# Hybrid attention and mixture-of-experts layer: the stretch from the first norm to the first expert's gate-up, rearranged

## Chip, core and metric

The kernel runs on one core of one Trainium2 chip. The metric is the device time of one execution in microseconds: 1241.69 is the median of three runs of the kernel before (1239.27 to 1242.06).

## The reference

One decoder layer over 256 tokens of width 1024, all in float32: a mixer of three attention kinds, a LayerNorm, 32 experts of which each token uses 4, and a LayerNorm. What matters here, cut down:

```python
mix = hybrid_mixer(x, ...)
x = layer_norm(DEEPNORM_ALPHA * x + mix, ln1_g, ln1_b)
logits = x @ router_w + router_b                     # 256 x 32
top_logit, top_e = lax.top_k(logits, 4)
top_w = softmax(top_logit)
for e in range(32):                                  # tokens routed to e
    gu = xb @ w_gu[e] + b_gu[e]                      # 1024 x 2048 weights, 8 MB
    gate, up = minimum(gu[:, :1024], 7), clip(gu[:, 1024:], -7, 7)
    y = (gate * sigmoid(1.702 * gate) * (up + 1)) @ w_dn[e] + b_dn[e]    # 4 MB
    out[tokens] += y * w[:, None]
x = layer_norm(DEEPNORM_ALPHA * x + out, ln2_g, ln2_b)
```

## The kernel before

The program is written by hand, one stream of instructions per engine with explicit semaphores; there is no scheduler. The tokens are two blocks b of 128. The five streams are SP (weight loads, from line 290), POOL (403), ACT (487), TensorE (712) and VectorE (1171). All of TensorE's products but a few pass through the helper at line 716 and its transposes through lines 723, 947, 964, 1048 and 1053, so that rows must be told apart by shape. A float32 product appears as two matmul instructions, a float32 transpose as one.

**Weights.** Two buffers hold gate-up weights (8 MB each, in four chunks of 2 MB, for even and odd experts), one holds down weights (4 MB, in four chunks). SP loads those of experts 0 and 1 ahead (line 326), as far as the buffers are free, the down weights of expert 0 after the last output projection (line 331), and then loops over pairs of experts: each chunk is loaded again when TensorE has used it (`guc`, `dn_used`), extra blocks included (`xguc`, `xdnc`, with an offset of four). Before the loop SP waits for the semaphore `routed`.

**Experts.** An expert takes up to 64 tokens in its slots. The products run over 64 stationary columns in two column groups. An expert with more tokens gets extra blocks of 32 slots, with 32 stationary columns in four column groups; the number per expert, `nx`, is computed on the chip. Expert 1 has one such block in this data.

**From the norm to the first gate-up** (the stretch of the change):

- The output projections give 12 pieces; VectorE adds each to `y` (`add_mixed`, line 1395), for block 0 up to piece 7, for block 1 up to piece 11. Pieces 8 and 10 belong to block 1's first half.
- `norm` (1411) takes statistics of both halves (1413, 1414), aggregates (1416), adds epsilon (1417), multiplies by the gain (1419) while POOL computes the power -1/2 (478, or 482 in the final norm), and applies deviation and bias (1421), which signals `x1ok`.
- TensorE transposes x block by block (947, eight each), ACT copies to `x1T` (609, two halves of a block). Then the router: eight products per block with x1T as the stationary operand (128 columns) and 32 moving columns, both blocks behind both blocks' transposes.
- VectorE clears `CTx` and `ysb` (1429, 1430) behind the norm. Per block it adds the bias (1436), finds the top 8 and their indices (1437, 1438), subtracts the maximum (1439; ACT then takes the exponential, 615), and makes a 0/1 mask (1440 to 1443).
- TensorE counts tokens per expert with five products of `before` and the mask (written to PB2).
- VectorE normalises the routing weights (1448 to 1452), computes `nx` in six operations from the counts (1457, 1460), then the slot number of each token (1463, 1464; `routed`), and the one-hots of experts 0 and 1: `oh`, and `ohw` with the routing weight (1473, 1474), eight operations, signalled by `ohs`.
- TensorE transposes the routing weights (964), gathers the tokens of experts 0 and 1 with 16 products (32 instructions) in two halves, clears the output accumulators with eight bf16 products of zeros, and starts the gate-up. ACT copies both halves of the gather (625); the gate-up waits for the second.
- After the first gate-up: activation on VectorE (1498 to 1504) and ACT (659), four transposes (1048), two of `ohw` (1053), and `combine`, the first product into the accumulators: bias of the down projection by routing weight.

## Time and profile before

| | |
|---|---|
| median of three runs | 1241.69 us |
| the profiled execution | 1241.96 us, of which span 1240.2 us |
| TensorE busy | 1101.1 us (89%) |
| VectorE busy | 266.9 us (22%) |
| ACT, POOL busy | 146.2 and 30.1 us |
| HBM read | 424.91 MB, 343 GB/s over the span |
| chain that ended last | TensorE 50%, transfers 29%, SP's queue 14%, VectorE 3%, issue 2% |

The page cuts the span into 40 slices of 31 us. A slice in which transfers move some 418 GB/s is one in which they are busy all the time; TensorE's 89% doesn't make it the bound there, since its matmuls wait within such a slice too. TensorE's granted clock has two levels here, 1.00 (2.4 GHz) and 0.50 (1.2 GHz); a stretch with a value between them has some of both. Ends of matmuls are modelled, so starts are read rather than ends where a row allows it.

### The profile page before, as it was taken

To read this page: it belongs to the slowest core of one execution; us is meant where nothing else is said; L and a number is where in the kernel's file an instruction comes from. 1 tells how busy PE (TensorE), PEld (TensorE's weight loads), DVE (VectorE), ACT (ScalarE), POOL (GpSimd) and SP (SyncE) were. 2 spreads that over 40 slices of the span, in tenths; PEclk is the share of its full clock that TensorE was granted. 3 is DMA by queue.
4 is the path that set the end of the run, shared out by engine and by line. 5 is a ranking of instruction groups with operands and counts; after the bars stand their busy time and mean duration, and the time that the engine had idled before them with its cause. 6 is when DMAs were issued, how large, how long until landed. Compare 5 with 4: busy or idle time off the path is not lost.

```text
span 1240.2 us, 14598 instructions
## 1 busy us (share of the span) xinstructions
PE 1101.1 (89%) x5388; PEld 474.5 (38%) x5389; DVE 266.9 (22%) x767; ACT 146.2 (12%) x309; POOL 30.1 (2%) x53
## 2 busy tenths in 40 slices
PE   7999796998899998989898878999989898989883
PEld 6677445333234332323232332433333232323221
DVE  2354535111112111121111111111211111111113
ACT  2144311100001000001000001001000010100000
POOL 3000410000000000000000000000000000000000
PEclk9999896998899999999999998999999999999997
DMA  9400849730999999999999958999999999999993
GB/s 314 181 1 1 262 191 393 294 137 17 419 419 418 419 418 418 418 417 417 418 419 418 418 232 326 418 417 418 417 418 418 418 418 418 419 418 418 417 414 120
DMA packets 80435, 426.32 MB, mean 344 GB/s; under 512 B 6025, under 2 KB 7610, under 8 KB 47610
## 3 DMA queue, kind: packets, MB, share of 16 engines
q1 hardware_dynamic: 79834, 425.37, 84.8%
q10 hardware_dynamic: 576, 0.61, 0.2%
q8 instruction: 16, 0.26, 0.1%
q14 instruction: 9, 0.07, 0.0%
HBM read 424.91 MB, written 1.05 MB: 343 GB/s over the span
## 4 chain that ended last, share of the span: by engine, by line
PE 50%; DMA 29%; SPq 14%; DVE 3%; issue 2%; ACT 1%; POOL 0%; DVEq 0%; POOLq 0%; ACTq 0%
PE PB L716 48%; DMA WB<-in_w_gate_up_dram 22%; SPq L331 6%; DMA WB<-in_w_down_dram 6%; SPq L326 6%; PE PB L1048 0%; DMA X<-in_x_dram 0%; SPq L335 0%; DVE S L1395 0%; PE PB L723 0%; DVE S L1524 0%; POOL K L478 0%; DVE WB L1289 0%; PE PB L806 0%; DVE S L1504 0%
## 5 line engine op out<-in xcount | busy, mean ns | idle before, releaser
L716 PE MATMUL PB<-WB,S 128*64 128x512 f32 (+5 forms) x3472 | 775.0, 596 | 72.3 <-DMA WB<-in_w_gate_up_dram 62.6
L716 PEld LDWEIGHTS PB<-WB,S 128*64 128x64 f32 (+2 forms) x3472 | 250.0, 140 | 562.8 <-issue 410.5
L1498 DVE TENSOR_SCALAR S<-PB 128x512 f32<-128x512 f32 (+1 forms) x34 | 23.5, 692 | 604.8 <-PE PB L716 604.8
L716 PE MATMUL PB<-S 32*64 32x512 f32 (+5 forms) x464 | 113.7, 594 | 4.9 <-issue 2.5
L659 ACT ACTIVATE S<-S 128x512 f32<-128x512 f32 x32 | 20.2, 630 | 556.4 <-DVE S L1498 556.4
L716 PE MATMUL PB<-S,X 128*128 128x128 f32 (+1 forms) x576 | 75.7, 293 | 9.3 <-DVE S L1524 8.0
L716 PEld LDWEIGHTS PB<-S,X 128*128 128x128 f32 x576 | 72.4, 208 | 23.7 <-issue 21.9
L716 PEld LDWEIGHTS PB<-S 32*64 32x64 f32 (+4 forms) x464 | 41.6, 164 | 65.0 <-issue 58.0
L1542 DVE COPY S<-PB 64x512 f32<-64x512 f32 x32 | 21.9, 683 | 205.4 <-PE PB L716 205.4
L716 PE MATMUL PB<-S,WB 128*128 128x256 f32 (+2 forms) x336 | 63.7, 391 | 0.4 <-ACT S L498 0.4
L716 PEld LDWEIGHTS PB<-S,WB 128*128 128x128 f32 (+1 forms) x336 | 49.5, 178 | 12.5 <-issue 2.1
L716 PE MATMUL PB<-WB 128*32 128x128 f32 (+7 forms) x260 | 44.7, 362 | 5.2 <-DVE WB L1362 3.3
L675 ACT ACTIVATE S<-PB 64x512 f32<-64x512 f32 x32 | 19.0, 593 | 203.0 <-PE PB L716 203.0
L716 PEld LDWEIGHTS PB<-WB 128*64 128x64 f32 (+2 forms) x260 | 27.5, 152 | 18.7 <-issue 13.7
L482 POOL TENSOR_TENSOR K<-K 128x1 f32<-128x1 f32 x2 | 3.0, 1511 | 1038.4 <-DVE K L1417 1038.4
L1048 PE MATMUL PB<-K,S 128*128 128x128 f32 x128 | 21.5, 292 | 4.7 <-DVE S L1504 2.9
L1048 PEld LDWEIGHTS PB<-K,S 128*128 128x128 f32 x128 | 13.7, 143 | 30.7 <-issue 26.9
L1501 DVE SCALAR_TENSOR_TENSOR S<-S 128x512 f32<-128x512 f32 (+1 forms) x34 | 23.5, 691 | 1.2
L1504 DVE TENSOR_TENSOR S<-S 128x512 f32<-128x512 f32 (+1 forms) x34 | 23.5, 691 | 1.2
L1499 DVE TENSOR_SCALAR S<-PB 128x512 f32<-128x512 f32 (+1 forms) x34 | 23.2, 682 | 0.1
L625 ACT ACTIVATE S<-PB 128x512 f32<-128x512 f32 x32 | 19.1, 597 | 32.7 <-PE PB L716 32.7
L1473 DVE TENSOR_SCALAR S<-K 128x64 f32<-128x64 f32 x68 | 17.1, 251 | 21.6 <-PE PB L1053 19.5
(199 smaller groups left out, 339.4 us busy)
## 6 DMA issues: line engine op xcount, KB each, us to landing
WB<-in_w_gate_up_dram SPq DMA_DIRECT2D x128, 2048.0 KB, 22.8
WB<-in_w_down_dram SPq DMA_DIRECT2D x128, 1024.0 KB, 23.0
WB<-in_w_in_dram SPq DMA_DIRECT2D x1, 3088.0 KB, 15.2
WB<-in_w_in_dram SPq DMA_DIRECT2D x1, 3072.0 KB, 20.3
WB<-in_w_in_dram SPq DMA_DIRECT2D x1, 2144.0 KB, 11.1
WB<-in_w_in_dram SPq DMA_DIRECT2D x1, 2048.0 KB, 16.1
WB<-in_w_out_dram SPq DMA_DIRECT2D x2, 1024.0 KB, 10.2
WB<-in_w_out_dram SPq DMA_DIRECT2D x1, 2048.0 KB, 16.7
```

The lines of the kernel that those rows point to most:

```text
L326: sp.dma_start(gu_slot[par][:, kk * c:kk * c + kk, :], src[:, kk * c:kk * c + kk, :]).then_inc(s_gul[par][c], 16)
L331: sp.dma_start(dn_slot[:, kk * c:kk * c + kk, :], src[:, kk * c:kk * c + kk, :]).then_inc(s_dnl[par][c], 16)
L625: act.activation(xg[:, 4 * h:4 * h + 4, :].rearrange("p k s -> p (k s)"), PB[bank][:, :], ACT.Copy)\
L659: act.activation(act_sb, gt, ACT.Sigmoid, scale=SWIGLU_ALPHA).then_inc(s["sig"], 1)
L675: act.activation(ysb[64 * e:64 * e + 64, 1, :], PB[7][64:128, :], ACT.Copy).then_inc(s["ysb_ok"], 1)
L716: return mm_(o, l, r, start=start, stop=stop, skip_group_check=True)
L1048: ins = tr(PB[bank][:, P * c:P * c + P], act_sb[:, P * c:P * c + P], ident)
L1498: ts(g, gate, LIMIT, None, ALU.min).then_inc(s[g_ok], 1)
L1499: ts(u, up, LIMIT, -LIMIT, ALU.min, ALU.max).then_inc(s[clip], 1)
L1501: stt(u, u, 1.0, g, ALU.add, ALU.mult).then_inc(s[upg], 1)
L1504: tt(a, u, a, ALU.mult).then_inc(s[done], 1)
L1542: cp(ysb[64 * e:64 * e + 64, 0, :], PB[7][0:64, :]).then_inc(s["ysb_dv"], 1)
```

## The change

**Norm.** The first half's statistics are taken before the last addition of a block (which only touches the second half), and the two wide operations are split into halves; `x1ok` is signalled per half, and TensorE transposes a half as soon as it is signalled. POOL's code serves both norms with one semaphore.

**Router.** Block 0's router stands before block 1's transposes. Weights are now the stationary operand (32 columns) and x1T moves (128 columns); k and k+4 accumulate in column group k, so that four partial sums of the transposed logits stand in four partition groups. ACT copies them (`lgT`), and one product with `fold`, four identities of 32 stacked, adds and transposes them back. VectorE builds `fold` at the start of the program with three additions.

**Routing.** VectorE signals the mask before it subtracts the maximum. It clears buffers between the two blocks. Three of the five count products are issued after block 0's mask. From the counts come first the slot numbers, for both blocks in two operations; then `oh` for both experts in one comparison, `ohs`; then `nx` (`nx_ok`), the routing weights (`wts_ok`), and `ohw` straight from `posm` and `wts`.

**Moved.** `ysb` is cleared by POOL. The transposes of the routing weights and the clearing of the accumulators stand behind the first gate-up, and ACT's copy of those weights behind its first sigmoid. The initial counts of `xguc` and `xdnc` come from the transposes. SP waits for `nx_ok` in place of `routed`.

```diff
@@ SP
-            sp.wait_ge(s["routed"], 1)
+            sp.wait_ge(s["nx_ok"], 1)
@@ POOL
...
+            for b in range(TB):
+                reciprocal_deviation(b)
+            pool.wait_ge(s["x1ok"], 2 * TB)
+            pool.memset(ysb, 0.0).then_inc(s["ysbz"], 1)
@@ ACT
+                act.wait_ge(s["lgp"], b + 1)
+                act.activation(lgT[:, b, :], PB[b][:, 0:P], ACT.Copy).then_inc(s["lgc"], 1)
+
+            act.wait_ge(s["ysbz"], 1)
+            act.dma_start(ysb[0:N_EXPERTS, :, :], b_dn[0].rearrange("e (h d) -> e h d", h=2)).then_inc(s["bdn_ld"], 16)
             for b in range(TB):
                 act.wait_ge(s["ract"], b + 1)
                 act.activation(lg[:, b, :], lg[:, b, :], ACT.Exp).then_inc(s["rsum"], 1)
...
             sigmoid(1)
+            act.wait_ge(s["wt_ps"], 1)
+            act.wait_ge(s["ctz"], 1)
+            act.activation(CT[0:N_EXPERTS, :, :].rearrange("p b t -> p (b t)"), PB[7][0:N_EXPERTS, 0:256],
+                           ACT.Copy).then_inc(s["ysb_ok"], 1)
             act_columns(5, 1)
             combine_weights(1)
+            act.wait_ge(s["nx_ok"], 1)
@@ TensorE
             for b in range(TB):
-                pe.wait_ge(s["x1ok"], b + 1)
-                if b == 1:
-                    pe.wait_ge(s["ymix"], 12)
                 for h in range(2):
+                    pe.wait_ge(s["x1ok"], 2 * b + h + 1)
+                    if b == 1 and h == 0:
+                        pe.wait_ge(s["ymix"], 12)
...
                     ins.then_inc(s["x1t"], 1)
-            for b in range(TB):
-                pe.wait_ge(s["x1tsb"], 2 * b + 2)
+                if b == 0:
+                    pe.wait_ge(s["ymix"], 11)
+
                 for k in range(KT):
-                    ins = mm(PB[b][:, 0:N_EXPERTS], x1T[:, k, P * b:P * b + P], rw[:, k, :], k == 0, k == KT - 1)
-                ins.then_inc(s["lgt"], 1)
-
-            pe.wait_ge(s["route"], 2)
+                    if k % 4 == 0:
+                        pe.wait_ge(s["x1tsb"], 2 * b + k // 4 + 1)
+                    q = 32 * (k % 4)
+                    ins = mm(PB[b][q:q + 32, 0:P], rw[:, k, :], x1T[:, k, P * b:P * b + P], k < 4, k >= 4)
+                ins.then_inc(s["lgp"], 1)
+                pe.wait_ge(s["lgc"], b + 1)
+                mm(PB[b][:, 256:256 + N_EXPERTS], lgT[:, b, :], fold, True, True).then_inc(s["lgt"], 1)
+
+            pe.wait_ge(s["route"], 1)
             mm(PB[2][:, 0:32], before[:, 0:P], msk[:, 0, :], True, False)
             mm(PB[2][:, 32:64], before[:, P:256], msk[:, 0, :], False, False)
+            mm(PB[2][:, 64:96], before[:, P:256], msk[:, 0, :], False, False)
+            pe.wait_ge(s["route"], 2)
             mm(PB[2][:, 32:64], before[:, 0:P], msk[:, 1, :], False, False)
-            mm(PB[2][:, 64:96], before[:, P:256], msk[:, 0, :], False, False)
             mm(PB[2][:, 64:96], before[:, P:256], msk[:, 1, :], False, True).then_inc(s["cntp"], 1)
...
             gate_up(0, 1, 1)
+            expert_weight_transposes()
+            clear_outputs()
             act_transposes(5, 1)
@@ VectorE
+            link(tt(fold, ident[:, 0:32], ident[:, 32:64], ALU.add))
+            link(tt(fold, fold, ident[:, 64:96], ALU.add))
+            tt(fold, fold, ident[:, 96:128], ALU.add).then_inc(s["foldok"], 1)
...
             for b in range(TB):
-                for n in ((6, 7), (8, 9, 10, 11))[b]:
+                for n in ((6,), (8, 9, 10))[b]:
                     add_mixed(n)
+                dve.wait_ge(s["ymix"], (7, 11)[b])
+                link(half_stats(y, b, 0))
+                add_mixed((7, 11)[b])
                 dve.wait_ge(s["ymix"], (8, 12)[b])
-                norm(y, None, b, "lnstat", "lnp", 48, lng, lnb, x_sb, "x1ok", "ln_ld")
-            dve.wait_ge(s["x1ok"], 2)
-            dve.memset(CTx, 0.0)
-            dve.memset(ysb, 0.0).then_inc(s["ysz"], 1)
+                link(half_stats(y, b, 1))
+                for ins in norm(y, b, b + 1, lng, lnb, x_sb, "ln_ld"):
+                    ins.then_inc(s["x1ok"], 1)
...
+            dve.wait_ge(s["x1ok"], 2 * TB)
+            route(0)
+            dve.memset(CTx, 0.0).then_inc(s["ctxz"], 1)
...
+            route(1)
+            dve.wait_ge(s["cntp"], 1)
             dve.wait_ge(s["route"], 2)
+            pm = posm[:, 0:N_EXPERTS, :].rearrange("p e b -> p b e")
+            link(stt(pm, PB[2][:, 0:2 * N_EXPERTS].rearrange("p (b e) -> p b e", b=TB), -NOT_ROUTED, msk, ALU.add, ALU.mult))
+            ts(pm, pm, NOT_ROUTED, None, ALU.add).then_inc(s["routed"], 1)
+            dve.wait_ge(s["routed"], 1)
+
+            tt(oh.rearrange("p b (e s) -> p b e s", e=2), iota_s.unsqueeze(1).unsqueeze(1).broadcast_to([P, TB, 2, SLOTS]),
+               posm[:, 0:2, :].rearrange("p e b -> p b e").unsqueeze(3).broadcast_to([P, TB, 2, SLOTS]), ALU.is_equal)\
+                .then_inc(s["ohs"], 1)
...
+            ins.then_inc(s["nx_ok"], 1)
```

## Rows read from the trace of the kernel before

**Rows 1.** The page's 40 slices of 31 us: transfers' busy tenths, and bytes moved.
```profile
DMA  9400849730999999999999958999999999999993
GB/s 314 181 1 1 262 191 393 294 137 17 419 419 418 419 418 418 418 417 417 418 419 418 418 232 326 418 417 418 417 418 418 418 418 418 419 418 418 417 414 120
```

**Rows 2.** Chain of waits, in order of time: start us, us, what.
```profile
423.33 27.92 DMA WB<-in_w_gate_up_dram
```

**Rows 3.** Timeline, weight loads that SP issues: start us, us issuing, queue, line.
```profile
178.77 2.63 SPq L326 DMA_DIRECT2D WB<-in_w_gate_up_dram  x5
...
307.05 6.41 SPq L326 DMA_DIRECT2D WB<-in_w_gate_up_dram  x4
```

**Rows 4.** Timeline, 182 to 220 us: start, us, engine, line, out<-in, shape, count [idle].
```profile
182.97 0.69 DVE L1413 BATCH_NORM_STATS2 K<-S 128x6 f32<-128x512 f32 x1
...
183.58 0.68 DVE L1414 BATCH_NORM_STATS2 K<-S 128x6 f32<-128x512 f32 x1
...
194.45 1.28 DVE L1421 SCALAR_TENSOR_TENSOR X<-S,K 128x1024 f32<-128x1024 f32 x1 [0.52 <-POOL K L478]
...
195.79 1.97 PE L947 MATMUL PB<-K,X 128*128 128x128 f32 x8 [5.91 <-DVE X L1421]
...
197.55 6.87 PE L716 MATMUL PB<-S 128*128 128x32 f32 x32
...
204.46 0.19 DVE L1436 TENSOR_TENSOR K<-PB,K 128x32 f32<-128x32 f32 x1 [1.70 <-PE PB L716]
...
206.23 2.34 PE L716 MATMUL PB<-K 128*128 128x32 f32 x10 [1.81 <-DVE K L1443]
...
208.68 0.19 DVE L1457 TENSOR_SCALAR K<-PB 128x32 f32<-128x32 f32 x1 [0.44 <-PE PB L716]
...
212.76 5.53 PE L716 MATMUL PB<-S,X 128*128 128x128 f32 x32 [1.35 <-DVE S L1474]
...
218.13 1.04 PE L716 MATMUL PB<-S 128*128 128x256 bf16 x8
...
218.33 0.60 ACT L625 ACTIVATE S<-PB 128x512 f32<-128x512 f32 x1 [1.19 <-PE PB L716]
...
219.10 13.95 PE L716 MATMUL PB<-WB,S 128*64 128x512 f32 x64
```

**Rows 5.** Timeline, other places: instructions of the shapes that the change adds.
```profile
37.89 3.69 PE L716 MATMUL PB<-WB 128*32 128x128 f32 x64
...
58.63 0.42 DVE L1275 TENSOR_TENSOR WB<-WB 128x256 f32<-128x256 f32 x1
...
128.79 0.74 POOL L458 MEMSET WB<- 128x768 f32 x1 [117.51 <-PE PB L716]
...
242.95 0.38 ACT L670 ACTIVATE S<-PB 128x256 f32<-128x256 f32 x1 [4.27 <-PE PB L716]
...
257.68 3.84 PE L716 MATMUL PB<-S,X 128*128 128x128 f32 x32
...
303.19 9.69 PE L716 MATMUL PB<-WB,S 128*32 128x512 f32 x64 [0.47 <-ACT S L638]
```

**Rows 6.** Timeline, end of the first gate-up, and the transposes behind it.
```profile
232.98 0.21 PEld L716 LDWEIGHTS PB<-S 32*64 32x64 f32 x8 [0.81 <-issue]
...
236.94 1.12 PE L1048 MATMUL PB<-K,S 128*128 128x128 f32 x4 [2.86 <-DVE S L1504]
```

**Rows 7.** Busy time by stretch; PEclk is the granted clock as a share.
```profile
core 0: us, PE busy (x) PEld busy (x) DVE busy (x) ACT busy (x) POOL busy (x), PEclk, DMA share, GB/s
...
191.00:193.00 2.00, 0.00 (x0) 0.00 (x0) 1.91 (x5) 0.07 (x1) 0.18 (x1) 0.86 1.05 434
...
205.00:207.00 2.00, 0.77 (x4) 0.77 (x4) 1.71 (x11) 0.23 (x1) 0.00 (x0) 0.50 1.02 426
...
215.00:217.00 2.00, 2.00 (x14) 2.00 (x13) 0.00 (x0) 0.45 (x1) 0.00 (x0) 0.66 1.02 403
...
238.00:242.00 4.00, 4.00 (x10) 2.01 (x9) 1.64 (x8) 0.60 (x1) 0.00 (x0) 0.72 1.00 418
```

**Rows 8.** Timeline, VectorE at the start of the program.
```profile
9.00 0.69 DVE L1182 COPY S<-PB 128x512 f32<-128x512 f32 x1 [1.01 <-PE PB L723]
```

More of the change, by code:

```diff
@@ L123, in hybrid_layer @@
         fg, fb = reg_a[:, 0:D], reg_a[:, D:2 * D]
-        K = sb("K", 1170)
+        K = sb("K", 1202)
         take = carver(K[:, :])
@@ L146, in hybrid_layer @@
         before = take(2 * P)
+        fold = take(N_EXPERTS)
         idx8 = sb("idx8", TB * 8, U32)
@@ L615, in _ @@
                 act.activation(lg[:, b, :], lg[:, b, :], ACT.Exp).then_inc(s["rsum"], 1)
-            act.wait_ge(s["ysz"], 1)
-            act.dma_start(ysb[0:N_EXPERTS, :, :], b_dn[0].rearrange("e (h d) -> e h d", h=2)).then_inc(s["bdn_ld"], 16)
-            act.wait_ge(s["wt_ps"], 1)
-            act.wait_ge(s["ysz"], 2)
-            act.activation(CT[0:N_EXPERTS, :, :].rearrange("p b t -> p (b t)"), PB[4][0:N_EXPERTS, 0:256],
-                           ACT.Copy).then_inc(s["ysb_ok"], 1)
             def slots_to_sbuf(h, bank, n):
@@ L1430, in _, with route @@
-            dve.memset(ysb, 0.0).then_inc(s["ysz"], 1)
-            dve.memset(posm[:, N_EXPERTS:, :], NOT_ROUTED)
-            dve.memset(wts[:, N_EXPERTS:, :], 0.0)
-            for b in range(TB):
+                link(half_stats(y, b, 1))
+                for ins in norm(y, b, b + 1, lng, lnb, x_sb, "ln_ld"):
+                    ins.then_inc(s["x1ok"], 1)
+            def route(b):
                 dve.wait_ge(s["lgt"], b + 1)
-                link(tt(lg[:, b, :], PB[b][:, 0:N_EXPERTS], rb, ALU.add))
+                link(tt(lg[:, b, :], PB[b][:, 256:256 + N_EXPERTS], rb, ALU.add))
@@ L1484, in next_expert_rows @@
                 expert_rows(e)
-            cp(curp, posm[:, 0:2, :].rearrange("p e b -> p (e b)")).then_inc(s["xact"], 1)
-            cp(curw, wts[:, 0:2, :].rearrange("p e b -> p (e b)"))
-            dve.memset(ecnt[:, 0:1], 0.0)
-            link(dve.memset(ecnt[:, 1:2], 1.0))
-            one_hots(0)
+            for e in range(2):
+                for b in range(TB):
+                    ins = ts(ohw[:, b, 64 * e:64 * e + 64], iota_s, posm[:, e, b:b + 1], wts[:, e, b:b + 1],
+                             ALU.is_equal, ALU.mult)
+            ins.then_inc(s["xact"], 1)
             expert_rows(0)
@@ L1591, in _ @@
                 link(ins)
-                norm(yf, None, b, "fin", "flnp", 32, fg, fb, yf, "fout", "ln2_ld")
+                half_stats(yf, b, 0)
+                link(half_stats(yf, b, 1))
+                for h, ins in enumerate(norm(yf, b, TB + b + 1, fg, fb, yf, "ln2_ld")):
+                    if h == 1:
+                        ins.then_inc(s["fout"], 1)
     return nc
```

111 lines of the change are left out of this document (63 added, 48 removed).

## Prediction

> **What bounds the kernel now.** I read the page's slices first. The bytes moved per slice stand at 417 to 419 GB/s from the eleventh slice (310 us) to the end, but for one dip, and at 294, 137 and 17 GB/s in slices 8 to 10 (217 to 310 us) [rows 1]. So the kernel has two regimes: a head in which the weight buffers are full and transfers wait for the engines, and a long tail in which the transfers set the pace. The chain of waits says the same: its first long piece that is a transfer of expert weights stands at 423.33, 27.92 us of gate-up weights [rows 2]; such pieces follow at every second expert, and ahead of it the long pieces are TensorE's. The question for an edit in the head is what starts the tail. SP's issues answer it: the prefetch of gate-up weights for experts 0 and 1 goes out at 178.77 (five chunks of 2 MB), and the load of expert 3, with which the unbroken stream begins, is issued at 307.05 [rows 3]. That load waits for TensorE's extra block of expert 1, whose gate-up starts at 303.19 [rows 5]. Between the first gather and that moment TensorE is in the chain throughout. Whatever brings the first gate-up forward by n us brings 307.05 forward by n, and the whole stream behind it.
>
> The stretch that the change touches runs from 182 to 219 us. In order of time: the first LayerNorm's statistics for token block 0 start at 182.97; the last operation of the norm for block 1 runs 194.45 to 195.73; eight transposes of block 1 take 195.79 to 197.76; the router's 32 matmul instructions run 1.97 to 6.87 us more (197.55 to 204.42); routing of block 1 on VectorE starts at 204.46; the count matmuls run from 206.23; VectorE then reads them at 208.68; the first gather starts at 212.76 and the first gate-up at 219.10 [rows 4]. TensorE was idle for 5.9 us, 1.8 us and 1.35 us before the transposes, the counts and the gather: this is a chain of dependences with short work on each engine, so durations on it count in full.
>
> **The norm.** Today both halves' statistics follow the last addition, 0.61 us apart (182.97 and 183.58 [rows 4]). The change takes the first half's statistics ahead of the last addition, which for block 0 waits for its output projection anyway: block 0 is done 0.6 us sooner. Block 1's additions follow on VectorE directly, so it inherits this; there a statistics operation merely swaps places with an addition and gets one wait of its own more, so I keep 0.5 us. Then the last operation is split in halves and the first half alone lets the transposes start: half of the 1.28 us [rows 4], 0.64. Start of block 1's transposes: 195.79 - 0.5 - 0.63 = 194.66. The other split operation waits for POOL's power in any case, and two halves 0.61 us apart cost what one whole does, so they are put at nothing.
>
> **The router.** Today block 0's router stands behind block 1's transposes on TensorE. The change puts it before them, in VectorE's norm of block 1, where TensorE sits idle for 5.9 us [rows 4]; it and its copy end near 193, so it leaves the path: half of 6.87 us. Block 1's router is on the path in a new form. Its 8 products become 16 instructions with 32 stationary and 128 moving columns, in four column groups. The nearest row in shape took 3.69 us for 64, 58 ns each, in two groups at the high clock [rows 5]. The granted clock here is the low level (0.50, that is 1.2 GHz, in 205 to 207 [rows 7]), so I take 115 ns each, 1.85 us. Bounds: no overlap at all, as for a 128-column transpose or today's router instruction, 0.215 us each (6.87/32), 3.4 us; from the four-group row, 9.69 us for 64 instructions of 512 columns [rows 5], a quarter of its 151 ns and doubled for the clock, 1.2 us. Changing the tile shape costs too: before the 32x64 matmuls the weight load stood for 0.81 us [rows 6], of which some 0.3 us are the pace of the stream itself, so I charge 0.5 us for the one switch between transposes and router; the switch to the fold lies under ACT's copy. Then come two steps that are new: ACT's copy of the partial sums (128x128; the 128x256 copy is 0.38 us [rows 5], I take 0.3), and the fold, one product of two instructions as today's router has them, 0.43 us. With a last instruction's 0.2 us and 0.05 us for a hand-over each: transposes to 196.63, switch to 197.15, router to 199.2 with its tail, copy to 199.55, fold to 200.25. ACT's x1T copies of 0.60 us [rows 4] run beside: the second half is there by 197.3, when TensorE is still at k 0 to 3. Today the result stands at 204.42, so 4.2 us are saved here, of which 1.13 come from the norm.
>
> The Trainium skill, page "TensorEngine Tiling (Array Packing)", section "Key Properties", says that a change of tiling mode drains TensorE, which speaks against this change with its two switches per block. The 0.81 us row agrees with it as to sign; by that rule alone both switches of block 1 would lie open, and the sum would be 0.5 us less favourable. The Trainium skill, page "TensorE: Matmul & The Clock Gate", section "Measured speedup vs the span model", has groups run side by side, with about 4 ns for each further one. The two-group row, 58 ns against the 120 ns of a full-width gather instruction of as many columns (3.84/32 [rows 5]), agrees for two; by that page four groups would need half of that again, block 1's router an estimated 0.9 us and not 1.85, and the sum would be 0.9 us better.
>
> **Routing.** VectorE takes 206.23 - 204.46 = 1.77 us from the logits to the mask today [rows 4]; the subtraction in the middle moves behind the mask, 0.15 us off: 200.3 + 1.62 gives 201.9. Of the ten count instructions, 2.45 us to VectorE's next step (208.68), six depend on block 0 alone and are issued beforehand; four remain: 2.45 - 6 x 0.215 = 1.16 us, to 203.1. Today 4.08 us follow between 208.68 and the gather: the chain of six overflow counts, positions in two pairs, two copies and eight one-hot operations. Of these the change leaves three ahead of the gather: two over 64 columns, near the 0.19 us of the 32-column row [rows 4], and one 128x256 comparison like the 0.42 us row [rows 5]; with hand-overs 0.95 us. Gather at 204.0, against 212.76: 8.8 us sooner. The memsets on VectorE between the blocks (0.5 us) lie in its wait for block 1's router, from about 197 to 200.
>
> **What is moved off.** The 4 KB-wide memset of ysb goes to POOL, idle here; 768 columns took it 0.74 us [rows 5]. ACT waits for it before it issues the b_down load and computes the exponentials. Queued behind are the gather's copies at 208, 11 us later; hidden. The routing weights (four operations per block), the overflow counts and the weighted one-hots now run under the gather and first gate-up (over 20 us). SP waits for the overflow counts rather than the positions, ready at about 205, and its next load needs the first gate-up chunk anyway. The eight clearing bf16 products (1.04 us) stood under ACT's copy of the gather's second half, so that their removal there gains nothing: the gate-up still follows that copy (218.33, 0.60 us; gate-up 219.10 [rows 4]). They and the two weight transposes now go behind the first gate-up, where TensorE waits for the activation up to 236.94 [rows 6], 2.8 us: about 1.5 us, hidden. ACT's copy of these weights falls between its sigmoid and the transposes. If that cover were gone they would cost 1.5 us once. They may also give something: in today's gap the clock falls, and 238 to 242 runs at 0.72 of the full clock [rows 7], so 2.2 us at the low level, a loss of 1.1 us; filled, the gap may keep the clock. Between 0 and 1.1 I take 0.5. The three fold additions at the start of the program shift VectorE by about 0.6 us, while its second copy waits 1.01 us for TensorE [rows 8]: nothing. The final norm is cut in halves also; nothing.
>
> **The sum.** 8.8 + 0.5 = 9.3 us. The weights don't take it back: the five chunks from 178.77 are 10 MB, some 25 us at 419 GB/s [rows 1, 3], and the first gate-up would start at 210.3, its last chunk's partner later still. The profiled execution took 1241.96 us, 1.8 us more than its span, and it gives 1232.7; it lies 0.3 us above the median of the runs, 1241.69. Predicted: 1232.5 us.
>
> **Rivals.** (a) The clock stays up. It was at 1.00 until 191 and fell after TensorE's idle time (0.86 in 191 to 193 [rows 7]); now TensorE has the router in that idle time. At the high level the transposes cost 1 us, router, fold and counts 1.7 us less, and the gather 3.84 us as the later one does [rows 5] and not 5.53: 4.3 us, so 1228.2. For it: the work moved in; against it: this work is thin, and the busy router of today, 6.87 us without a pause, didn't raise the clock. 18%. (b) The router gains little: instructions one after the other, 1.6 us more, the rise of the clock after the gather and not in it (32 x 0.215 - 5.53 = 1.35 us), and no gain in the gap, 0.5: 3.5 us, 1236.0. Today's clock rose in the gather (215 to 217 at 0.66 [rows 7]), against it. 15%. (c) The end doesn't move, since transfers set it: 1241.7. Against it stands the idle time of the transfers in slices 8 to 10. 3%. (d) Slower: the thinned stretch leaves the clock at the low level well into the expert products. Each us of gate-up at that level loses 0.5; to eat the 9.3 us it would have to last 19 us, and 24 us to be slower by the 2.5 us that can be told. With 30 us it gives 1247.5. The rise in the gather within 4 us speaks against it. 2%. That leaves 62% for the forecast.
>
> **Numbers.** (a) and (b) together give 1228.2 to 1236; the worst of the unknown costs in (b) plus the clearing products uncovered, 1.5 us, give 1237.5. The range is 1228 to 1237.5, which leaves out (c), (d) and rare sums. Under 0.2% (2.5 us, about what a measurement of this kernel tells from no change): forecast, (a) and (b) are faster, 95%; (c) 3%; (d) 2%.
>
> **What to look at.** Block 1's transposes at 194.7; 32 router instructions of 32 stationary columns, near 0.115 us; fold near 200; gather at 204.0; gate-up 0 at 210.3; expert 3's first load at 298; span 1231. Wrong if the gather comes after 206, or if it comes in time and 307.05 moves by less than it.

## The result, and the profile after

The changed kernel takes 1225.86 us (median of 4 executions, 1225.25 to 1226.71), the kernel before 1240.48 in the same series. The ratio is 0.9883, with an interval of 0.9866 to 0.99: 14.6 us less. Forecast were 9.3 us less, 1232.5, with a range down to 1228.0. The direction was right, the size was not, and the time lies below the range.

The profiled execution took 1225.68 us, its span 1223.9, against 1240.2. Its page, the slices of 30.6 us:

```profile
DMA  9400759834999999999999939999999999999993
GB/s 315 187 1 1 231 206 386 332 139 181 418 418 417 418 417 418 417 418 417 418 418 418 418 144 409 417 418 417 418 418 417 419 417 418 418 418 418 418 414 122
```

The picture is that of [rows 1]. The stream still runs unbroken at 417 to 419 GB/s from the eleventh slice, with one dip; only what lies ahead of it has become shorter. The timeline of the changed stretch, from the last addition of block 0 (start us, us, engine, line, out<-in, shape, count, idle time and its releaser):

```profile
181.26 0.75 DVE L1426 SCALAR_TENSOR_TENSOR S<-PB,K,S 128x512 f32<-128x512 f32 x1 [0.29 <-PE PB L726]
...
189.74 0.82 PE L726 MATMUL PB<-S 128*32 128x128 f32 x16 [0.84 <-ACT S L616]
...
190.96 1.41 DVE L1453 SCALAR_TENSOR_TENSOR S<-S,K 128x512 f32<-128x512 f32 x2
...
191.12 0.99 POOL L483 TENSOR_TENSOR K<-K 128x1 f32<-128x1 f32 x1 [6.89 <-DVE K L1449]
...
192.40 1.42 DVE L1458 SCALAR_TENSOR_TENSOR X<-S,K 128x512 f32<-128x512 f32 x2
...
193.21 1.88 PE L958 MATMUL PB<-K,X 128*128 128x128 f32 x8 [1.84 <-DVE X L1458]
...
195.01 0.20 PEld L726 LDWEIGHTS PB<-S 128*32 128x32 f32 x8 [0.33 <-ACT S L616]
...
195.02 1.41 PE L726 MATMUL PB<-S 128*32 128x128 f32 x16
...
196.49 0.28 ACT L620 ACTIVATE S<-PB 128x128 f32<-128x128 f32 x1 [0.77 <-PE PB L726]
...
196.82 0.41 PE L726 MATMUL PB<-K,S 128*128 128x32 f32 x2 [0.40 <-ACT S L620]
...
197.34 0.19 DVE L1473 TENSOR_TENSOR K<-PB,K 128x32 f32<-128x32 f32 x1 [1.39 <-PE PB L726]
...
198.96 0.63 PE L726 MATMUL PB<-K 128*128 128x32 f32 x4 [1.06 <-DVE K L1479]
...
200.12 0.42 DVE L1497 TENSOR_TENSOR S<-K 128x256 f32<-128x256 f32 x1
...
200.60 5.25 PE L726 MATMUL PB<-S,X 128*128 128x128 f32 x32 [1.01 <-DVE S L1497]
...
206.53 13.95 PE L726 MATMUL PB<-WB,S 128*64 128x512 f32 x64 [0.69 <-ACT S L630]
...
224.36 0.66 PE L1065 MATMUL PB<-K,S 128*128 128x128 f32 x4 [1.66 <-DVE S L1560]
...
254.29 0.66 PE L1065 MATMUL PB<-K,S 128*128 128x128 f32 x4
...
291.09 6.30 SPq L328 DMA_DIRECT2D WB<-in_w_gate_up_dram  x4
```

The row at 193.21 answers to 195.79 of [rows 4], the one at 197.34 to 204.46, the gather at 200.60 to 212.76, the gate-up at 206.53 to 219.10, the row at 224.36 to 236.94 of [rows 6], and the load of expert 3 at 291.09 to 307.05 of [rows 3]. Cut at such landmarks, the two profiled executions and a second one of each kernel (first two runs of the next section) compare as follows, in us:

| stage | forecast gain | before | before again | after | after again |
|---|---|---|---|---|---|
| start to last addition, block 0 | 0 | 182.19 | 182.07 | 181.26 | 180.77 |
| to block 1's transposes | 1.13 | 13.60 | 13.60 | 11.95 | 11.95 |
| to VectorE's reading of the logits | 3.03 | 8.67 | 8.67 | 4.13 | 4.44 |
| to the gather | 4.6 | 8.30 | 8.30 | 3.26 | 3.70 |
| to the first gate-up | 0 | 6.34 | 6.36 | 5.93 | 6.35 |
| first bias product to second gate-up | 0.5 | 9.79 | 9.81 | 8.18 | 9.88 |
| down 0 to the next gate-up | 0 | 9.49 | 9.53 | 7.60 | 7.60 |
| final norms, first to last wide operation | 0 | 11.96 | 11.96 | 11.53 | 11.53 |

Of the stages left out, the first gate-up takes 13.89 in all and the way from the second gate-up to down 0 18.67; from the gate-up behind down 0 to expert 3's load it is 36.1, 36.1, 36.2 and 37.0, and from that load to the end 933.2, 932.8, 932.8 and 930.5. The first row of the table is luck: it lies between 177.7 and 182.3 over the profiled executions of all versions. The differences that return in both pairs are 1.65 + about 4.4 + about 4.8 + 1.9 + 0.4 = 13.2 us; the gap behind the first gate-up gives 1.6 more in one pair and nothing in the other. The first gate-up also starts 0.4 us sooner after the gather in the first pair (the clock), and in the second pair the stage ahead of expert 3's load takes 0.8 more. So between the last addition of block 0 and expert 3's load the first pair gains 15.0 us and the second 11.5; of the second pair's 15.1 us in all, 3.6 lie ahead of and behind the chain that was changed. Two things stand out against the forecast: the router gives more than 3.0, and 1.9 us vanish between down 0 and the next gate-up, where the change has touched nothing.

Two stretches of the changed kernel (start and end, length, busy us and count on PE, PEld, DVE, ACT and POOL, granted clock, transfers' share, GB/s):

```profile
201.00:203.00 2.00, 2.00 (x11) 2.00 (x11) 1.73 (x12) 0.00 (x0) 0.00 (x0) 0.50 1.01 371
...
226.00:230.00 4.00, 4.00 (x15) 1.43 (x15) 0.97 (x5) 0.38 (x1) 0.00 (x0) 1.00 1.01 420
```

The gather still runs at 1.2 GHz for its first half, as before; behind the gap, where the kernel before stood at 0.72 [rows 7], it is at 2.4 GHz now.

### The profile page after: what moved, and what is told of

Same layout as the page of the kernel before. It is cut to its first block, busy times and chain, and to the rows that moved or that the text cites. A ratio compares the mean times of both kernels' runs of the same rounds, so it can differ in the third digit from the quotient of the medians.

```text
span 1223.9 us, 14619 instructions
## 1 busy us (share of the span) xinstructions
PE 1094.2 (89%) x5392; PEld 466.8 (38%) x5393; DVE 266.5 (22%) x770; ACT 146.8 (12%) x311; POOL 29.2 (2%) x54
## 4 chain that ended last, share of the span: by engine, by line
PE 48%; DMA 28%; SPq 17%; DVE 4%; issue 2%; ACT 1%; DVEq 0%; ACTq 0%
PE PB L726 47%; DMA WB<-in_w_gate_up_dram 23%; SPq L333 9%; SPq L328 6%; DMA WB<-in_w_down_dram 5%; DMA X<-in_x_dram 0%; PE PB L1065 0%; DVE S L1453 0%; DVE K L1443 0%; SPq L337 0%; DVE S L1426 0%; PE PB L733 0%; DVE S L1580 0%; DVE S L1645 0%; DVE WB L1320 0%
## 5 line engine op out<-in xcount | busy, mean ns | idle before, releaser
L726 PE MATMUL PB<-S 32*64 32x512 f32 (+5 forms) x464 | 107.7, 588 | 5.8 <-issue 2.5
L726 PEld LDWEIGHTS PB<-S 32*64 32x64 f32 (+5 forms) x464 | 34.9, 149 | 66.6 <-issue 58.3
L630 ACT ACTIVATE S<-PB 128x512 f32<-128x512 f32 x32 | 19.1, 597 | 32.7 <-PE PB L726 32.7
L548 ACT ACTIVATE WB<-WB 128x128 f32<-128x128 f32 (+1 forms) x40 | 17.7, 443 | 26.7 <-DVE WB L1322 26.7
## 6 DMA issues: line engine op xcount, KB each, us to landing
WB<-in_w_out_dram SPq DMA_DIRECT2D x1, 2048.0 KB, 16.3
```

The source lines that it names most:

```text
L630: act.activation(xg[:, 4 * h:4 * h + 4, :].rearrange("p k s -> p (k s)"), PB[bank][:, :], ACT.Copy)\
L726: return mm_(o, l, r, start=start, stop=stop, skip_group_check=True)
```

## The experiments

**Both kernels again.** No edit.

> The kernel before, once more, for a second trace. My account of the 16.3 us by which the two spans differ has two kinds of terms. If the kernel before is as in its first trace by design, this one shows again: TensorE idle for 1.8 us after the first down product (the 'issue' idle at 268.54), POOL's power at 1.51 to 1.53 us, the gap behind the first gate-up with a granted clock below 1 after it, 8.7 us from the end of the first gate-up to the second. If a term is luck of one execution, it differs here: I expect that of the first 182 us (0.9 us between the two traces) and of the moment at which the clock rises in the gather.

> The changed kernel once more. By design: POOL's power at 0.99 us, no idle of 1.8 us after the first down product, clock 1.00 through the gap behind the first gate-up, 7.1 us from the end of the first gate-up to the second. Luck: where the clock falls and rises between 190 and 206 us; the router of block 1 (1.41 us) and the gather (5.25 us) may come out up to 1 us longer or shorter.

They took 1241.53 and 1226.41 us; the stages are in the table. The stall and the norm come back to 0.05 us, the gap does not: the second execution of the changed kernel shows the low clock there.

```profile
225.00:229.00 4.00, 3.96 (x10) 2.45 (x11) 1.77 (x10) 0.60 (x1) 0.00 (x0) 0.57 1.01 420
```

Here the transposes, from 225.04, and the first products run at the low clock: from the first transpose to the second gate-up it is 5.93 us, against 4.24 in the first execution of the same kernel. So whatever the filled gap does for the clock, it does not do it in each execution.

**The gap's work alone, and taken away.** The kernel before with the eight clearing products moved behind the first gate-up (the initial counts that they signalled come from the transposes of x, as in the changed kernel):

```
...
             gate_up(0, 1, 1)
+            clear_outputs()
             act_transposes(5, 1)
```

> The kernel before with one edit: the eight clearing bf16 products stand behind the first gate-up, in the gap in which TensorE waits for the activation. Theory (the filled gap keeps the clock up): granted clock 1.00 from 234 to 242, the time from the end of the first gate-up to the start of the second falls from 8.7 to 7.1 us, the kernel gains 1.6 us (0.13%). Rival (the clock after the gap hangs on where in time the gap falls, and the products only fill idle time): 8.7 us stay, no gain. Rival 2: they are too thin, as today's router was, clock below 1.

Measured: 1241.83 us, ratio 0.9987 (0.9971 to 1.0003), gap 9.87. And the changed kernel with the clearing products ahead of the gather; the two weight transposes stay in the gap:

```
+            clear_outputs()
...
             expert_weight_transposes()
-            clear_outputs()
```

> The changed kernel with the eight clearing products back in front of the first gate-up, beside ACT's copy; the two weight transposes stay in the gap. Theory (the filled gap keeps the clock): the granted clock falls in or after the gap, end of first gate-up to second takes 8.5 to 8.7 us and not 7.1, the kernel is 1.5 us slower than the changed one. Rival (the two transposes are enough, or the gap's place decides): 7.1 us stay and the time is the changed kernel's within 0.3 us.

Measured: 1227.95 us, 0.9882 (0.9866 to 0.9898), gap 9.63. The stretch after the gap, in the first and then in the second kernel:

```profile
235.00:239.00 4.00, 4.00 (x10) 2.46 (x11) 1.69 (x9) 0.60 (x1) 0.00 (x0) 0.57 1.01 422
```

```profile
224.00:228.00 4.00, 3.83 (x10) 2.40 (x11) 1.89 (x11) 0.60 (x1) 0.00 (x0) 0.61 1.00 418
```

Neither part keeps the clock up alone. The forecast for the first of the two fell; what was left open was whether more work would do it in that kernel. A longer fill was therefore put into the kernel before, with ten products more whose result nobody reads:

```
 mm(acc(b, h)[:, 256 * q:256 * q + 256], zeros[:, 0:P], zeros[:, 0:256], q == 0, False)
+for _ in range(10):
+    mm(PB[6][:, 0:256], zeros[:, 0:P], zeros[:, 0:256], True, True)
```

> The kernel before with the eight clearing products behind the first gate-up, and ten more like them without use after them, so that TensorE has some 2.3 us of work in the 2.9 us of waiting for the activation. With the eight alone (1.0 us) the time between the two gate-ups stayed at 9.87 us. Theory (a well filled gap keeps the clock, eight were too few): 8.2 us, clock 1.00, the kernel 1.6 us faster than before. Rival (the change holds the clock there by something else, such as the moment at which the gap comes): 9.8 us.

```profile
234.00:238.00 4.00, 3.42 (x13) 1.99 (x14) 2.31 (x11) 0.60 (x1) 0.00 (x0) 1.00 1.02 424
```

Full clock, a gap of 8.20 us instead of 9.8, and 1237.97 us against 1240.73 for the kernel before on that chip: 0.9974 (0.9964 to 0.9983), 2.8 us faster although TensorE does more. Over all traces: the gap measured 9.63 to 9.89 us in all seven in which it held one of the two groups alone or none. Of nine traces of versions that hold both, seven show 8.18 to 8.20, and two of the plain changed kernel 9.87 and 9.88. The long fill has one trace.

**The stall behind down 0.** In the kernel before, the conditional for expert 0's extra block follows the down products and is jumped over. Its chain of waits there (start us, us, what), in order of time:

```profile
261.52 7.02 PE PB L716 x32
268.54 1.81 issue
270.35 0.66 PE PB L1048 x4
```

TensorE waits 1.81 us for nothing that the profile knows. The queue view of 1 us stretches names a candidate: within 267 to 268, as the down products end, one packet of 16 KB (0.02 MB; packets, MB, share) arrives on a queue that carries instructions; the page of the changed kernel has 17 of them in all, 0.28 MB.

```profile
q8 instruction: 1, 0.02, 6.2%
```

In the changed kernel such packets arrive in 248 to 249 and 253 to 254, the first beginning 6 us before the jump at 254.3. The theory: what counts is where the jump lies in TensorE's code, and the change moved it by changing the number of instructions ahead. Three versions of the kernel before test it, two with empty instructions at the start of TensorE's program and one with 24 tiny products (48 instructions), whose result nobody reads:

```
+for _ in range(8):          # 32 in the second
+    pe.nop()
```

> The kernel before with 8 empty instructions at the start of TensorE's program, where TensorE waits 6 us for x anyway. Both traces of the kernel before have TensorE idle for 1.8 us after the first down product (9.49 and 9.53 us from that product to the gate-up behind it), both of the changed kernel have not (7.60). Theory (where TensorE's code lies decides, since the branch over the first skipped extra block finds its code not yet loaded): moving the code by 8 instructions can take the 1.8 us away, to 7.6. Rival (something the change does to other engines or to nx): 9.5 us stay whatever is put in front.

> As with 8 empty instructions, with 32. Theory: the stall depends on the number; with at least one of 8 and 32 it is gone or another length. Rival: 9.5 us in both.

```
+w = ident.bitcast(BF16)
+for _ in range(24):
+    mm(PB[5][:, 0:32], w[:, 0:P], w[:, 0:32], True, True)
```

> The kernel before with 24 tiny bf16 products into an unused bank at the start of TensorE's program, in its 5 us of waiting for x: they move all its later code by 48 instructions. The 8 and 32 empty instructions left the stall as it was (9.60 and 9.50 us from the first down product to the gate-up behind it). But they may have left no trace in the code: the code load by the transfer engines that falls into the last of the down products came 6 us after the first of them in all these kernels, and 1 us after it in the changed kernel, 6 us ahead of the branch. Theory (the code load is asked for where the stream crosses a border, and the branch comes too soon behind it): with 48 real instructions the load comes earlier in the down products and the stall is gone: 7.6 us. Rival (the stall comes from elsewhere): 9.5 us.

The empty instructions changed nothing, against the forecast: 1240.42 and 1242.41 us, stall and work together 9.60 and 9.50. Whether they stand in the loaded code at all, no run shows. The real instructions did it: the stage takes 7.61. The time, 1241.06 us, is that of one execution and shows no gain: the kernel before lay between 1236.27 and 1244.7 in that series. The transposes behind the jump, second execution of the kernel before, then the version with 24 products:

```profile
270.30 0.66 PE L1048 MATMUL PB<-K,S 128*128 128x128 f32 x4 [1.86 <-issue]
```

```profile
268.09 0.66 PE L1051 MATMUL PB<-K,S 128*128 128x128 f32 x4
```

A packet now arrives already in 260 to 261, 7 to 8 us before the jump:

```profile
q8 instruction: 1, 0.02, 8.1%
```

The long fill shifted the code by 20 instructions and lost the stall as well (7.61, packets at 258 and 264, jump at 264.5). That fits a gain of more than the 1.6 us expected of it. Over all seventeen traces: the five with the wait have no such packet in the 20 us ahead of the jump but the one that comes as the down products end; the twelve without it have another one 5.2 to 10.6 us ahead. So 1.9 us of the changed kernel's gain come, in its stages, from nothing that the change is meant to do, but from where one conditional lies in TensorE's program. That the wait is one for code is read from these packets; the shift by real instructions is what the experiments show. The Trainium skill, page "Runtime: NRT & Kernel Launch", section "Instruction fetch mechanics", says that code comes in blocks of 16 KiB and that a taken branch to a place outside what is loaded has to wait for the fetch. The packets of 0.02 MB and the 1.8 us at the jump agree; that page has no figure for such a wait.

The wait can cost more than itself. In three of the five traces with it (the short fill, 8 and 32 empty instructions) the clock falls just behind it, and the 64 instructions of the next gate-up take 15.6 us and not 13.95. With 8 empty instructions:

```profile
268.00:272.00 4.00, 4.00 (x16) 1.42 (x17) 0.00 (x0) 0.60 (x1) 0.00 (x0) 0.66 1.03 410
```

**The norm.** The changed kernel with each wide operation of the norm in one piece:

```
-for h in range(2):
-    c = slice(512 * h, 512 * h + 512)
-    ins = stt(v[:, b, c], v[:, b, c], st[:, o:o + 1], g[:, c], ALU.subtract, ALU.mult)
-link(ins)
+link(stt(v[:, b, :], v[:, b, :], st[:, o:o + 1], g, ALU.subtract, ALU.mult))
...
```

> The changed kernel with the norm's two wide operations whole, 1024 columns, and x1ok per block; the statistics stay split around the last addition. Theory (POOL's power cannot start or finish while a VectorE operation on SBUF runs, so it ends 0.4 us behind that operation): the power takes 1.52 us again and not 0.99; last addition of block 0 to block 1's transposes 13.0 us and not 11.95; about 1.1 us slower from there on. Rival (the 0.5 us of the power come from POOL's own code, which the change also rewrote): power 0.99 us, transposes at 12.6.

and with the first of them in four pieces (`range(4)`, 256 columns):

> The changed kernel with the first wide operation in four quarters of 256 columns. Theory (the power ends 0.4 us behind the VectorE operation that runs when it starts): the power takes about 0.7 us, as for the root mean squares. Rival (0.99 is its own length): it stays at 0.99. In either case VectorE's own four quarters set the next step, so the transposes of block 1 start no earlier than 11.95 us after the last addition, at most 0.2 later.

Whole: 1226.24 us, 0.9905 (0.9869 to 0.9942). Quarters: 1227.23 us, 0.9908 (0.9875 to 0.9941). As times they can't be told from the changed kernel, since the executions of each spread over several us; the stages can. From the last addition to the transposes it takes 13.40 us whole, 12.46 in quarters and 11.95 in halves; 13.0 and at most 12.15 were expected. For the whole version the trace shows why: VectorE stands idle for 0.48 us between its first two additions of block 1,

```profile
182.50 0.74 DVE L1426 SCALAR_TENSOR_TENSOR S<-PB,K,S 128x512 f32<-128x512 f32 x1
183.72 1.64 DVE L1426 SCALAR_TENSOR_TENSOR S<-PB,K,S 128x512 f32<-128x512 f32 x2 [0.48 <-DVE S L1426]
```

where the other sixteen traces have these additions without a pause, 0.34 us closer. What made this pause is open; without it the stage is 13.06, as expected. VectorE's operation and POOL's power beside it, whole and then quarters:

```profile
187.95 1.27 DVE L1451 SCALAR_TENSOR_TENSOR S<-S,K 128x1024 f32<-128x1024 f32 x1
...
188.11 1.52 POOL L483 TENSOR_TENSOR K<-K 128x1 f32<-128x1 f32 x1 [6.92 <-DVE K L1449]
```

```profile
189.05 1.66 DVE L1453 SCALAR_TENSOR_TENSOR S<-S,K 128x256 f32<-128x256 f32 x4
...
189.21 0.72 POOL L483 TENSOR_TENSOR K<-K 128x1 f32<-128x1 f32 x1 [7.42 <-DVE K L1449]
```

POOL's one-column operation takes 1.52, 0.99 or 0.72 us. In the whole version it ends 0.41 us after VectorE's operation; with pieces of 0.70 and 0.41 us it ends 0.45 and 0.47 us after the piece that was running when it began. Halving the operation thus shortens the wait for POOL, from 189.63 - 187.95 = 1.68 us after the start of the wide operation to 1.15; VectorE's own two pieces, 1.41 us, then end last. From start to start, the next wide operation follows after 1.44 us and not 1.78, twice over, since block 1's norm stands behind block 0's; the next operation itself, in two pieces, costs block 0 0.13 us more. That is 0.56 us in all. In quarters POOL is quicker still, but nobody waits for it any more, and the four pieces take 1.66 us, 0.25 more per block, which is the 0.5 us by which quarters lie behind halves. The Trainium skill, page "GPSIMD Engine Reference", section "Specifications", has POOL share its way into SBUF with VectorE and lists operations with two SBUF inputs as those that contend; this one has two, and the lengths agree.

**The router in its old form.** The changed kernel's order, with the router as one product per k of 128 stationary columns, without copy and fold:

```
-q = 32 * (k % 4)
-ins = mm(PB[b][q:q + 32, 0:P], rw[:, k, :], x1T[:, k, P * b:P * b + P], k < 4, k >= 4)
...
+ins = mm(PB[b][:, 256:256 + N_EXPERTS], x1T[:, k, P * b:P * b + P], rw[:, k, :], k == 0, k == KT - 1)
```

> The changed kernel with each block's router in its old form (x1T stationary, 32 moving columns, the logits at once, no copy and no fold), the order of the change kept. From block 1's transposes to its logits the changed kernel takes 4.13 and 4.44 us. Theory of the prediction, corrected by the trace (16 instructions of 32 stationary columns are far cheaper than 16 of 128): the old form takes 3.4 us at the low clock where the new takes 1.4 us, 0.3 for the copy and 0.4 for the fold: about 5.5 us in all, 1.2 us slower than the changed kernel. Rival (the order alone brings the gain): 4.4 us or less.

```profile
194.58 3.62 PE L724 MATMUL PB<-S 128*128 128x32 f32 x16
```

1227.27 us, 0.9893 (0.9869 to 0.9918). Transposes to logits 5.50 us, as expected, against 4.13 and 4.44 in four groups, 8.67 before. So of the 4.4 us that this stage gained, 3.2 come from block 0's router being done earlier. The form gives 1.1 at the same low clock (5.50 against 4.44); the 0.3 us more of the first execution come with the clock, which rises there at the fold.

**The overflow counts back ahead of the one-hots.**

```
-pm = posm[:, 0:N_EXPERTS, :].rearrange("p e b -> p b e")
...
 ins.then_inc(s["nx_ok"], 1)
+pm = posm[:, 0:N_EXPERTS, :].rearrange("p e b -> p b e")
...
```

> The changed kernel with the six overflow counts ahead of the slot numbers again, the rest of its order kept. From block 1's logits to the gather: 3.26 us in the changed kernel at the high clock, 3.70 at the low one. Theory (the order counts in full, six operations of 0.22 us): 1.3 us more, 4.6 to 5.0 us, and the kernel 1.3 us slower. Rival (VectorE has slack here since the gather waits for something else): no more than 0.3 us.

```profile
197.66 0.19 DVE L1494 TENSOR_SCALAR K<-PB 128x32 f32<-128x32 f32 x1 [1.00 <-PE PB L726]
...
199.38 0.42 DVE L1506 TENSOR_TENSOR S<-K 128x256 f32<-128x256 f32 x1
```

1226.97 us, 0.9881 (0.9859 to 0.9904). From VectorE's first step after the counts to the one-hots 1.72 us; logits to gather 4.92, 1.22 more than the 3.70 of the executions with the low clock there. The stage carries the price, the total does not show it against the spread of the clock's luck.

**Useless products wherever TensorE waits.** How much is left in the clock? The changed kernel with small bf16 products whose result nobody reads, 12 behind block 0's router, 6 before the counts of block 1 and 6 before the gather:

```
 mm(PB[2][:, 64:96], before[:, P:256], msk[:, 0, :], False, False)
+busy(6)     # mm(PB[7][:, 0:256], w[:, 0:P], w[:, 0:256], True, True), six times
 pe.wait_ge(s["route"], 2)
```

> The changed kernel with small bf16 products without use in TensorE's idle stretches: 12 behind block 0's fold, 6 before it waits for the mask of block 1, 6 before it waits for the one-hots. Theory (what TensorE does in these stretches decides whether the clock falls): granted clock 1.00 from 190 to the first gate-up; block 1's eight transposes 1.04 us and not 1.88, its router 0.8 and not 1.4, the gather 3.84 and not 5.25 to 5.66; first gate-up 2.5 us earlier than in the changed kernel. Rival (thin work doesn't hold the clock, as the old router didn't raise it): clock 0.50 before the gather, no gain, at most 0.2 us lost.

1225.12 us, 0.9874 (0.9855 to 0.9893), with executions from 1217.33 to 1226.7. The profiled one, 1217.33, stands at 1.00 from 189 to 226; the other five have a mean granted clock of 0.971 or 0.972, like the changed kernel's, against its 0.980. Its span is 8.4 us below that of the changed kernel's first trace, and not all of this is the clock: 3.0 us lie ahead of block 0's last addition, 3.6 behind expert 3's load and only 1.9 between them. Then more of them, 5 ahead of block 0's router, 3 behind each, then 15, 8 and 8, beside the changed kernel on one chip:

> The changed kernel again, on the chip of the other two, to compare them in the same hour. Theory: 1224 to 1227 us; last addition to transposes 11.95, logits to gather 3.26 or 3.70, first down product to the next gate-up 7.60 us; end of the first gate-up to the second 8.2 (six of seven traces with both groups of instructions in that gap so far had it) and not 9.8 as in all traces with less there.

> The changed kernel with more products without use than in the earlier experiment (5 before block 0's router, 3 before each fold, 15 after block 0's, 8 and 8 before the mask and the one-hots), so that TensorE has hardly an idle stretch from the last projection to the first gate-up. The earlier one held the clock in its trace and ran at 1217.3, but its other five executions lay at 1222.3 to 1226.7. Theory (the fall hangs on how full the idle stretches are, and 12, 6 and 6 were at the edge): the clock is held in most executions, median 1219 to 1222 against 1225 to 1226 for the changed kernel. Rival (the one fast execution was luck in other places too): median as the changed kernel's, within 1.5 us, or slower by up to 1 us where the products stand in front of the router.

The changed kernel took 1225.27 us there, 0.9875 (0.9857 to 0.9893), the filled one 1221.6, 0.9845 (0.9824 to 0.9867): it beats both kernels, by 3.7 us and 19.1, and its five executions (1217.53 to 1223.74) all lie below the changed kernel's four (1225.13 to 1230.23). By the mean clock three of the five kept it up (0.975 to 0.978) and two did not (0.970 and 0.971). The second half of its router, its gather and 2 us within the gather, and then 2 us within the gather of the changed kernel in that series, which starts at 202.36:

```profile
195.69 0.43 PE L726 MATMUL PB<-S 128*32 128x128 f32 x8 [0.23 <-ACT S L616]
...
200.30 3.84 PE L726 MATMUL PB<-S,X 128*128 128x128 f32 x32
```

```profile
201.00:203.00 2.00, 2.00 (x21) 2.00 (x20) 1.70 (x12) 0.60 (x1) 0.00 (x0) 1.00 1.00 391
```

```profile
203.00:205.00 2.00, 2.00 (x11) 2.00 (x11) 1.72 (x12) 0.00 (x0) 0.00 (x0) 0.50 1.01 418
```

At 2.4 GHz the gather takes 3.84 us, where the changed kernel has 5.25 to 5.67; the way from the transposes to the logits takes 3.34 against 4.44, and the gap 8.19 against 9.87 in the changed kernel's profiled execution of that series.

## Why the prediction was off

**What bounds the kernel** held. Expert 3's load came 15.96 us earlier (307.05 to 291.09), the span 16.3. From that load to the end both profiled executions take the same within 0.4 us: what was won ahead of the stream arrived at the end. Over all seventeen traces the load comes between 286.3 and 308.2 us, and the rest takes 929.3 to 933.8. Rivals (c) and (d) are out by this.

**The norm** was priced at 1.13 us and gave 1.65. The step that failed is "the other split operation waits for POOL's power in any case": the power was taken as fixed, and it depends on VectorE's operation, 1.52 us beside 1024 columns and 0.99 beside 512. The two terms that the sum had came out as priced. The early statistics save 0.56 us (block 0's first wide operation starts 1.82 us after its last addition and not 2.42; block 1 gives 0.04 back), and block 1's transposes start 0.81 us after the last wide operation and not 1.34, which saves 0.53. The halved first operation gives the 0.56 us that the sum lacked. (The whole version took 13.40 against 13.60, which looks as if the statistics gave 0.2 only; 0.34 of it is the pause on VectorE.) The same effect gives 0.4 us in the final norms, which the sum had at nothing.

**The router** was priced at 3.03 us and gave 4.2 to 4.5. Its mechanism held (block 0's router went into the idle time, 189.74 to 190.56; wide form against groups as expected). Its sizes did not. The 16 instructions took 1.41 us and not 1.85, although the granted clock was 0.50 all through them (195 to 196.4), so the step that failed is the price of 115 ns each, taken from the row of two groups. Narrow views of the changed kernel (to 195.2, to 195.5, from 195.95) show the 16 as two bursts of eight, from 195.02 and 195.77:

```profile
195.02 0.44 PE L726 MATMUL PB<-S 128*32 128x128 f32 x4
...
195.02 0.66 PE L726 MATMUL PB<-S 128*32 128x128 f32 x8
...
195.12 0.60 ACT L616 ACTIVATE S<-PB 128x512 f32<-128x512 f32 x1 [0.26 <-PE PB L958]
...
195.77 0.20 PEld L726 LDWEIGHTS PB<-S 128*32 128x32 f32 x8 [0.55 <-ACT S L616]
...
195.77 0.65 PE L726 MATMUL PB<-S 128*32 128x128 f32 x8
```

Four instructions, one per column group, take 0.44 us and the next four only 0.22 more: 54 ns each, so that the four groups together take as long as one full-width instruction (0.215 us). At the high clock (the filled version above) it is 0.32 us for the first four of a burst and 0.43 for eight, so 28 ns each by the modelled ends; by the starts, 195.03 and 195.16, it is 33. The second burst waits for ACT's copy of the second half of x, which ends at 195.72; the products are not what sets its start. The estimate by the Trainium skill, page "TensorE: Matmul & The Clock Gate", section "Measured speedup vs the span model", was 0.9 us for these 16. The pace of 54 ns agrees with it (16 x 54 ns = 0.86 us); the rest of the 1.41 is the wait for the copy and the tail of each burst. The 0.5 us for the switch isn't there: the router follows the transposes at once (193.21 + 1.88 = 195.09, router 195.02), and the weight load's idle time names ACT's copy, 0.33 us. The 0.81 us of [rows 6] returns before the 32x64 matmuls of the changed kernel too, but it is no price for this switch. Here the drain told of in the Trainium skill, page "TensorEngine Tiling (Array Packing)", section "Key Properties", does not show as a cost.

**Routing** was priced at 4.6 and gave 5.04 and 4.60. Right; the difference between the two executions is the clock in the four count instructions, 0.63 us in the first and 1.06 in the second.

**The gap** was priced at 0.5 out of 0 to 1.1, and gave 1.6 in seven of nine. That a filled gap keeps the clock was the right reason. The failed step is taking half of a gain that came either whole or not at all, and reading the loss from the four us from 238 of [rows 7] only: the low clock had begun before them, with the transposes. The whole of it costs 1.6 us and not 1.1.

**The stall** is not in the prediction: the sum left it at nothing without a reason. It stood in the chain of waits of the kernel before as 1.81 us of "issue", and I read that chain for its long pieces. Whether an edit removes or creates such a wait can't be foreseen from the trace alone, but that 1.9 us stood open there could be read, and would have widened the range.

**Rival (a)**, 1228.2 with the clock up, came nearest in time but not in mechanism: the changed kernel's clock does fall, to 0.50 in the gather. What (a) described exists: the gather of 3.84 us, in the filled version.

Put together: the forecast was short by 0.5 (norm), 1.4 (router), 0.2 (routing), 1.1 (gap), 1.9 (stall) and 0.4 us (final norms), 5.5 us, against 14.6 - 9.3 = 5.3 measured. That the two agree so closely is in part luck: the list takes the gap at its full gain, which two traces of nine don't have, and single executions differ by more than it is off. All the errors had the same sign. The range took each unknown only at its dear end, and had no room below for a cheap router, the whole gap and the stall together.

**What stays open.** Why two executions of the changed kernel lose the clock in a filled gap and seven traces of it and its versions don't; why some executions lose it behind the stall. Whether empty instructions count in loaded code. The parts of the norm, the router's form and the counts in the total time: they are shown in their stages, not in medians.

## What to carry to other kernels

Ahead of a stream that later sets the pace, every us on the chain of dependences is a us of the end, so read that chain to its short pieces, "issue" among them: behind a conditional it can be the wait for code. When work is moved into TensorE's waits, ask not only whether it leaves the path, but also what it does to the clock: here products that compute nothing made the kernel faster still. And an operation that waits for POOL while VectorE runs a long one beside it is cheaper in two pieces; four were slower than two.

## What the runs showed of the hardware that was not expected

- A wait of 1.8 to 1.9 us on TensorE at a jumped-over conditional came and went with 20 or 48 instructions more ahead of it, with a packet of 16 KB on an instruction queue as the products ahead of it end (wait, five traces) or another 5.2 to 10.6 us ahead of the jump (no wait, twelve traces). In three of the five the clock then fell and the next gate-up took 15.6 us and not 13.95.
- A one-column operation on POOL took 1.52, 0.99 or 0.72 us beside VectorE operations of 1024, 512 or 256 columns.
- fp32 instructions of 32 stationary and 128 moving columns in four column groups: four more add 0.22 us at the low clock, 54 ns each, where a full-width instruction takes 0.215 us there; in two groups they take 58 ns each at the high clock [rows 5].
- The 6.87 us of router instructions with 32 moving columns left the granted clock at 0.50 [rows 7]; 42 bf16 products of 256 columns in the waits kept it at 1.00 from 178 to 210 us in the profiled execution, and by the mean clock in three of five.
